# Pooling sums moved behind their matrix product, squares summed on the tensor engine, row roots on GpSimd, and eight FFN weight units kept for both token halves

## The reference, cut to what matters

```python
gate = sigmoid(rms_norm(h, g_ple) @ w_ple_gate + b_ple_gate)     # 512 tokens, 1024x1024
h = h + gate * (p @ w_ple_proj)                                  # 256x1024
hs = concat(meta_tokens, h)                                      # 16 + 512 = 528 tokens
h = rms_norm_2(hs, norm_mix_pre[0])
# pool_mixer: 4 channel groups of 256, windows W = 2, 4, 8, 16
cs = cumsum(h);  p_g = (cs - cs shifted by W) / count - h        # over the tokens
mix = concat(p_g @ w_groups[g]) * scale                          # 4 products 256x256
hs = hs + rms_norm_2(mix, norm_mix_post[0])
h = rms_norm_2(hs, norm_ffn_pre[0])
hs = hs + rms_norm_2((silu(h @ w_gate) * (h @ w_up)) @ w_down, norm_ffn_post[0])   # 1024 -> 2816 -> 1024
```

## Time and profile before

| | |
|---|---|
| median of 3 runs | 2180.49 us (2180.46 to 2183.39) |
| the profiled execution | 2178.2 us, its span 2176.1 us |
| PE busy | 1931.7 us, 89% of the span |
| DVE / ACT / POOL busy | 1001.9 / 659.5 / 205.9 us |
| granted TensorE clock, mean | 0.942 of full speed |

### The profile page before, as it was taken

One profiled execution on the slowest core, in us unless ns is written; L12 is line 12 of the kernel. 1 busy time (PEld: TensorE's weight loads), 2 busy tenths in 40 slices (PEclk: granted clock), 3 DMA queues, 4 the chain that ended last, 5 costly groups with the idle time before them and its releaser, 6 DMA issues.

```text
span 2176.1 us, 32437 instructions
## 1 busy us (share of the span) xinstructions
PE 1931.7 (89%) x13854; PEld 1649.0 (76%) x13854; DVE 1001.9 (46%) x1798; ACT 659.5 (30%) x1215; POOL 205.9 (9%) x205
## 2 busy tenths in 40 slices
PE   5987999949999989988569999997988969999997
PEld 4754788836665656668569999997856759999996
DVE  5744334342333322347884422447655485322456
ACT  5333323211100010034443222234454543222232
POOL 0021000000000000001230000003122240000012
PEclk9998999959999999998779999998989979999998
DMA  4211243539999999941114232233301224232242
GB/s 151 87 40 56 82 142 139 207 151 406 426 425 425 426 425 426 425 196 59 31 57 146 88 102 84 88 117 108 106 30 59 78 83 141 98 107 84 92 140 84
DMA packets 59236, 359.92 MB, mean 165 GB/s; under 512 B 6432, under 2 KB 9120, under 8 KB 46800
## 3 DMA queue, kind: packets, MB, share of 16 engines
q1 hardware_dynamic: 55120, 344.22, 41.6%
q0 software_dynamic: 3504, 12.73, 1.6%
q10 hardware_dynamic: 464, 0.85, 0.1%
HBM read 353.58 MB, written 4.19 MB: 164 GB/s over the span
## 4 chain that ended last, share of the span: by engine, by line
PE 68%; DVE 12%; DMA 10%; ACT 5%; POOL 2%; issue 2%; SPq 0%; POOLq 0%; DVEq 0%; ACTq 0%
PE bank L402 49%; DMA e<-in_we 9%; PE bank L587 7%; PE bank L609 4%; ACT SS L2184 1%; POOL zacc L2292 1%; PE bank L448 1%; PE bank L620 1%; DVE ztmp L1494 1%; DVE wlo L988 1%; PE bank L621 1%; DVE scr L1151 1%; DMA B<-in_rel 1%; DVE SS L1631 1%; DVE sm L1638 1%
## 5 line engine op out<-in xcount | busy, mean ns | idle before, releaser
L402 PE MATMUL bank<-nhi,whi 128*128 128x256 f32 (+2 forms) x1568 | 457.4, 292 | 21.9 <-DVE nlo L1504 7.7
L402 PE MATMUL bank<-nlo,whi 128*128 128x256 f32 (+2 forms) x1568 | 451.8, 288 | 0.0
L402 PE MATMUL bank<-nhi,wlo 128*128 128x256 f32 (+2 forms) x1568 | 451.6, 288 | 0.0
L988 DVE TENSOR_TENSOR wlo<-raw,whi 128x1024 fp32r<-128x1024 f32 x259 | 323.6, 1255 | 138.8 <-ACT whi L1745 135.0
L402 PEld LDWEIGHTS bank<-nhi,whi 128*128 128x128 f32 x1568 | 302.2, 193 | 28.0 <-issue 13.6
L1745 ACT CAST whi<-raw 128x1024 fp32r<-128x1024 f32 x259 | 269.4, 1042 | 121.7 <-PE bank L402 101.4
L402 PEld LDWEIGHTS bank<-nhi,wlo 128*128 128x128 f32 x1568 | 301.6, 192 | 1.6
L402 PEld LDWEIGHTS bank<-nlo,whi 128*128 128x128 f32 x1568 | 301.9, 193 | 1.0
L587 PE MATMUL bank<-e,xT 128*64 128x256 f32 x2048 | 237.1, 385 | 1.0 <-DVE xT L1280 1.0
L587 PEld LDWEIGHTS bank<-e,xT 128*64 128x64 f32 x2048 | 143.1, 138 | 83.0 <-issue 12.8
L402 PE MATMUL bank<-ghi,whi 128*128 128x256 f32 (+1 forms) x704 | 201.1, 286 | 0.0
(11 more groups left out here) (281 smaller groups left out, 2837.0 us busy)
## 6 DMA issues: line engine op xcount, KB each, us to landing
e<-in_we SPq DMA_DIRECT2D x96, 2048.0 KB, 36.6
raw<-in_w_down SPq DMA_DIRECT2D x64, 512.0 KB, 3.4
raw<-in_w_gate SPq DMA_DIRECT2D x52, 512.0 KB, 3.4
raw<-in_w_up SPq DMA_DIRECT2D x52, 512.0 KB, 3.5
raw<-in_w_q SPq DMA_DIRECT2D x12, 512.0 KB, 4.5
B<-in_rel POOLq DMA_DIRECT2D x8, 512.0 KB, 4.2
raw<-in_w_gc SPq DMA_DIRECT2D x8, 512.0 KB, 4.0
raw<-in_w_ga SPq DMA_DIRECT2D x8, 512.0 KB, 4.3
```

The source lines that it names most:

```text
L402: i = e.matmul(o, a, x[:, k0 + k, c0:c1], start=(k == 0 and n == 0), stop=(k == j.K - 1 and n == 2))
L988: e.tensor_tensor(wlo[wslot(u)][:], raw[u % NRAW][:], whi[wslot(u)][:].bitcast(F32), ALU.subtract).then_inc(*hit("dve_low", ("lo", u)))
```

## The change

It does these things:
- **Windows behind the product.** `pw` now multiplies the split of `hT` times the gain, without the factor; DVE applies the factor to the product on its way out of PSUM (`scaled_products`), and makes the window sums of the product into `yT` (`windows`). The window sums are linear, so the result is the same; `pool_scale` goes into the gain of the following norm (`gp`).
- **An explicit order** of 16 gate tiles j on all engines, without a break between the halves, with the pooling products of half 0 after tiles 12 to 15 (PSUM banks 4, 5, 6 in turn; bank 7 takes column sums).
- **Squares on TensorE** for `ple` 0, `pre0` 1, `mp0` and `fp0` (`SUMMED`): `square_sum` multiplies each block's squares by ones, one matmul per block and chunk, in place of the additions on POOL and the closing `columns`. POOL still adds for `ple` 1 and `pre0` 0.
- **Root on POOL** for all eight norms here (`root_of`), with the mean made by ACT (`mean`).
- **Weights kept**: the 8 units of the first FFN tiles are loaded and split once and used by both halves (`SLOT`, twelve slots); half 1's `fg`, `fu` are the same jobs as half 0's.
- **Post of `mp0`** in both halves is a block of its own (`mixed_post`) with all adds on DVE; `pe_open` writes out the order of the first FFN tiles. Two table loads of ACT are placed ahead of their use (`warm`). The spread of the last expert pair comes after `pp` tile 1, not 3.

```diff
-                if m == 3:
-                    pe_spread(NP - 1, range(8), w, pool=SIDE)
-            side.add(pe_norm("ple", 0, 4, 6))
-            side.add(nothing(8))
-            side.add(pe_norm("ple", 1, 4, 6))
...
+                if m == 1:
+                    pe_spread(NP - 1, range(8), w, pool=(4, 5, 2, 3, 6, 7))
+                if m > 4:
+                    for k in (2 * m - 10, 2 * m - 9):
+                        square_sum("ple", 0, k)
+            side.add(sums("ple", 0, (6, 7)))
+            for j in range(16):
+                r, m = j // 8, j % 8
+                tile(J["pg"], m, ("pg", m, r), phi[r], plo[r], [(0, (0, 256))], lambda k: [("pn", k, r)], keep=(r == 0))
+                if j == 0:
+                    side.drain()
+                if j == 1:
+                    spread("ple", 0)
+                if j == 5:
+                    columns("ple", 1)
+                if j == 7:
+                    side.add(spread_in(3, "ple", 1))
+                if j == 8:
+                    side.drain()
+                if j == 10:
+                    columns("pre0", 0)
+                if j > 10:
+                    square_sum("pre0", 1, j - 11)
+                if j == 11:
+                    side.add(spread_in(3, "pre0", 0))
+                if j == 12:
+                    side.drain()
+                if j >= 12:
+                    pool_products(0, (2 * j - 24, 2 * j - 23), REST)
...
         def pe_pool():
-            columns("pre0", 1)
...
+            for k in range(5, 8):
+                square_sum("pre0", 1, k)
+            pool_products(1, range(4), DENSE)
+            pool_products(1, (4, 5), REST)
+            spread("pre0", 1)
+            for k in range(8):
+                square_sum("mp0", 0, k)
+            pool_products(1, (6, 7), DENSE)
+            spread("mp0", 0)
+
+        def pe_open():
...
             for r in range(2):
+                side.add(sums("fp0", r, range(4 * r, 8)))
+                for i in range(FIRST):
+                    tile(J["fg", 0, i, r], 0, ("fg", 0, i, r), nhi, nlo, [(r, RG[r])], lambda k: [("n", "fp0", r, k)],
+                         keep=(r == 0))
+                    side.drain()
+                    tile(J["fu", 0, i, r], 0, ("fu", 0, i, r), nhi, nlo, [(r, RG[r])], lambda k: [], keep=(r == 0))
+                    if i == 0:
+                        spread("fp0", r)
+                    if r == 0 and i == 1:
+                        for k in range(8):
+                            square_sum("mp0", 1, k)
+                    if r == 0 and i == 2:
+                        spread("mp0", 1)
+                    if r == 0 and i == 3:
+                        for k in range(4):
+                            square_sum("fp0", 1, k)
+
+        def square_sum(nm, r, k):
...
+            for x, c in chunks:
+                n = MT if x == 0 and k else 128
+                p = e.matmul(b[0:n, x:x + 1], sq[:, c - c0:c - c0 + n], ones[:, 0:1], start=(k == 0 and x == chunks[0][0]),
+                             stop=(k == 7 and x == chunks[-1][0]))
...
+            for m in (2 * g, 2 * g + 1):
...
+                e.tensor_tensor(zn[:, m, MT:MT + n], bk("pw", m, r, 0, n=n), rb[:, c0:c1], ALU.mult).then_inc(
+                    *hit("dve_win", ("free", "pw", m, r, 0)))
...
+        def dve_pool():
             for g in range(4):
+                scaled_products(1, g)
+            windows(1, 0)
+            windows(1, 1)
+            mixed_post(0)
+            windows(1, 2)
+            windows(1, 3)
+            feed(U_FFN + 4)
...
         def act_pool():
+            mean("pre0", 1)
+            feed(U_FFN + 2)
+            pooled_squares(0, range(4))
             rb_copy("pre0", 1)
+            pooled_squares(0, range(4, 8))
+            mean("mp0", 0)
+            feed(U_FFN + 4)
+            mixed_post(0)
+            mean("fp0", 0)
+            pooled_squares(1, range(4))
+            rb_copy("fp0", 0)
...
+        def root_of(nm, r):
...
+            e.tensor_scalar(y.bitcast(I32), xm.bitcast(I32), -0.5, 1597463007.0, ALU.mult, ALU.add).then_inc(*hit("pool_root"))
+            for n in range(3):
+                w.wait_ge(*last("pool_root"))
+                e.tensor_tensor(u, y, y, ALU.mult).then_inc(*hit("pool_root"))
+                w.wait_ge(*last("pool_root"))
+                e.tensor_tensor(u, u, xm, ALU.mult).then_inc(*hit("pool_root"))
+                w.wait_ge(*last("pool_root"))
+                e.tensor_scalar(u, u, -0.5, 1.5, ALU.mult, ALU.add).then_inc(*hit("pool_root"))
+                w.wait_ge(*last("pool_root"))
+                e.tensor_tensor(y, y, u, ALU.mult).then_inc(*hit("pool_root"))
...
+            for i in range(m0, n1):
+                e.tensor_scalar(dg[:, i - 1, :], ident, rcol[:, 0, i:i + 1], None, ALU.mult).then_inc(
+                    *hit("pool_root", *([("diag", nm, r)] if i == n1 - 1 else [])))
...
+        for nm, r in (("ple", 0), ("ple", 1), ("pre0", 0), ("pre0", 1), ("mp0", 0), ("fp0", 0), ("mp0", 1), ("fp0", 1)):
+            if (nm, r) not in SUMMED:
+                for k in range(1, 7):
+                    accumulate(nm, r, k)
+            root_of(nm, r)
```

More of the change, by code:

```diff
@@ L687, in nothing, with spread_in @@
                 yield
-        def pe_pool():
-            columns("pre0", 1)
-            for r in range(2):
-                for m in range(8):
-                    tile(J["pw"], m, ("pw", m, r), nhi, nlo, [(0, RG[r])], lambda k: [("win", k, r)],
-                         k0=2 * (m // 2), keep=(r == 0))
-                    if r == 0 and m == 3:
-                        spread("pre0", 1)
-                if r == 0:
-                    side.add(pe_post("mp0", 0))
-            side.drain()
+        def spread_in(n, nm, r):
+            yield from nothing(n)
+            spread(nm, r)
+            yield
@@ L701, in columns, with sums @@
+        def sums(nm, r, ks):
+            for k in ks:
+                square_sum(nm, r, k)
+                yield
         def columns(nm, r):
             c0 = RNG[nm][r][0]
-            b = take(("col", nm, r), SIDE)
+            b = take(("col", nm, r), (7,) if nm in ("ple", "pre0") else SIDE)
             w.wait_ge(*at("acc", nm, r, 6))
             w.wait_ge(*at("sq", nm, r, 7))
-            sq = zlast[marks.noted("last", nm, r)]
+            sq = zq[marks.noted("sq", nm, r, 7)]
             for x, c in CH[r].items():
@@ L716, in spread @@
             m0 = max(n0, 1)
-            b = take(("rb", nm, r), SIDE)
+            b = take(("rb", nm, r), REST if nm in ("ple", "pre0", "mp0", "fp0") else SIDE)
             o = MT if n0 == 0 else 0
@@ L742, in pe_ffn @@
             rdy = [lambda k, r=r: [("n", nev, r, k)] for r in range(2)]
-            for r in range(2):
+            if l == 0:
+                pe_open()
+            for r in range(2) if l else ():
                 for i in range(FIRST):
@@ L910, in tensor @@
         pe_pool()
-        side.add(pe_norm("fp0", 0, 2, 4))
-        side.add(pe_post("mp0", 1))
-        side.add(pe_norm("fp0", 1, 2, 6))
         pe_ffn(0, RG, 0, "fp0", pe_after0)
@@ L922, in _program, with span @@
     WAIT = 10
+    SUMMED = [("ple", 0), ("pre0", 1)] + [(n, r) for n in ("mp0", "fp0") for r in range(2)]
+    def span(r):
+        return RG[r]
     LAG = (4, 6)
@@ L1446, in win_low @@
[L1446 to L1468 removed]
+            n = c1 - c0
@@ L1735, in scalar @@
         fed, nsq = [0], [0]
[L1736 removed]
+        sq_user = {}
         def feed(top):
@@ new lines, in act_ple, with act_gate_step @@
+            for i in (15, 16):
+                act_gate_step(i)
+            e.activation(warm[:], epst[:], ACT.Silu).then_inc(*hit("act_route"))
+        def act_gate_step(i):
+            if i < 16:
+                sigmoid(i % 8, i // 8)
+            if 0 <= i - 1 < 16:
+                k, r = (i - 1) % 8, (i - 1) // 8
+                c0, c1 = span(r)
+                w.wait_ge(*at("h ple", k, r))
+                e.activation(nhi[:, k, c0:c1], hT[:, k, c0:c1], ACT.Copy, scale=v1("mix_pre", k)).then_inc(
+                    *hit("act_norm", ("win hi", k, r)))
+                square("pre0", r, k, hT)
@@ L2030, in act_pool, with pooled_squares, mixed_post @@
+        def pooled_squares(r, ks):
+            for k in ks:
+                w.wait_ge(*at("pooled", k // 2, r))
+                square("mp0", r, k, yT, v1("pool_scale", k))
+        def mixed_post(r):
+            rb_copy("mp0", r)
+            for _ in post_steps("mp0", r, "fp0", ("ffn_pre", 0), 0):
+                pass
         def act_pool():
+            mean("pre0", 1)
+            feed(U_FFN + 2)
+            pooled_squares(0, range(4))
             rb_copy("pre0", 1)
-            side.add(nothing(8))
@@ L2033, in act_pool @@
-            for m in range(8):
-                tile(J["pw"], m, cap=J["pw"].u0 + 1)
-                c0, c1 = RG[0]
-                w.wait_ge(*at("out", "pw", m, 0))
```

(16 more changed lines are left out.)

461 lines of the change are left out of this document (231 added, 230 removed), and 4 rows, old and new, of the table k.

## The result

The changed kernel takes 2165.98 us (median of 4 runs, 2163.63 to 2166.57), the kernel before 2180.47 us (4 runs, 2178.53 to 2183.39) beside it. The ratio is 0.993, with a 95% interval from 0.9913 to 0.9948. It is faster, by 14.5 us; the forecast was 43 us, and its range ended at 2163. One execution of the kernel before (4774.87 us, beside experiments 1 to 4) and one of experiment 3 (3981.70 us) fell in another, much slower state of the chip and are in no figure here.

The account below looks back on a forecast made before the run. TensorE's stream bounds the kernel outside a hole of idle time and half clock. Milestones won 51.5 us at full clock, less 8 clock loss: 43.5 off 2178.2 is 2134.7, written as a 2138 us median; range 2120 to 2163.

Parts of the forecast that it names:

- the forecast's milestones: PE's predicted times: `pg` 974.1, end of `pw` half 0 1033, first FFN tile 1055.5, first tiles done 1121 at full clock.
- its clock loss of 8: Half clock in parts from 1033 to 1066 costs 3 to 14 us, taken as 8.
- the 8 where I had the cover end: `ple` 1 and `mp0` 1 have three tiles of cover, gone from about 8 us a root on.
- The forecast's waits of PE for diagonals: PE's waits for roots up to the first 528-token tile: 1, 1.7, 3.2, 2 and 1 us.
- the price of the root: A root on POOL: small instructions at 0.25 us each, 4 us in all, between bounds of 3.2 and 9.7.
- its count of six places: Six roots stand in PE's way: `ple` 0, `pre0` 0 and 1, `mp0` 0, `fp0` 0 and 1.
- it keeps the clock up: The added square matmuls, 18.5 us at full clock, land much in idle time of PE and keep its clock up.
- the upper bound: POOL's root at large-addition pace: 13 instructions at 0.61 us and 3 diagonals at 0.6, 9.7 us.
- the forecast's own rule: Each us more in a root on POOL costs 6 us, for six roots in PE's way.
- The rival on the slow POOL: Small POOL instructions cost like large ones, 0.61 us, root 9.7 us: 2180 us, no gain; chance 0.09.
- the post of `mp0` paces `fg` 0: In the first FFN tile, DVE's three instructions a block set the pace: 1.17 us a block, 9.4 in all.
- Worth nothing themselves: The eight weight units less save no time themselves, since PE never idles after 1136.9 us.

Follow-up runs that it names:

- experiments 1 to 4: Changed kernel with, in turn: one Newton step, 2148.15 us; roots back on DVE, 2161.96; squares of `mp0`, `fp0` added on POOL, 2168.87; column sums left out, 2154.56.
- experiment 3: Changed kernel with the squares of `mp0` and `fp0` added on POOL again, roots left there: 2168.87 us.
- after: The changed kernel itself, as timed beside the kernel before: 2165.98 us, ratio 0.993.
- experiment 1: Changed kernel with one Newton step instead of three in POOL's eight roots: 2148.15 us.
- experiment 4: Changed kernel without the column matmuls of blocks 1 to 6 in `mp0` and `fp0`: 2154.56 us.
- Number 7: Changed kernel with one Newton step in POOL's roots and the column sums of blocks 1 to 6 in `mp0`, `fp0` left out: 2138.03 us.
- experiment 8: Changed kernel with ScalarE's reciprocal square root and diagonals in place of mean, root and diagonals on POOL: 2150.30 us.
- number 9: Changed kernel with roots on ScalarE, and six norms' sums made with ones standing still and squares moving: 2128.48 us.
- experiment 5: Changed kernel with 16 unused matmuls ahead of each of four PE waits for a diagonal: 2163.02 us.
- experiment 6: Changed kernel with the kept weights undone, 8 units loaded, subtracted and cast again for half 1: 2174.0 us.

## Why the prediction was right in kind and wrong in size

Here are the forecast's milestones and those of the traces (start of `pg`, last `pw` matmul of half 0, start of the first FFN tile, start of the first 528-token tile; us of the span; the forecast's last with its clock loss of 8), and the medians:

```
kernel                     pg      pw half 0   first FFN   528-token   median
forecast                   974.1   1033        1055.5      1129        2138
after                      976.5   1046.7      1081.5      1162.8      2165.98
1, one Newton step         975.3   1038.2      1064.6      1141.3      2148.15
4, sums left out           975.1   1045.3      1075.0      1150.0      2154.56
7, both                    975.2   1038.1      1061.0      1131.3      2138.03
8, root on ScalarE         976.4   1040.5      1064.6      1145.4      2150.30
9, wide sums too           974.9   1037.1      1057.9      1125.4      2128.48
```

**Right.** The waits for POOL's additions went, and with them the windows between `scaled` steps. DVE's steps are fast with POOL's additions away, as the forecast took from the earlier trace rows: a post's split of 128x272 takes 0.49 us in number 9. PE's two waits for DVE are as forecast: 3.8 us for the first post (4 with the copy) and 2.2 for a bank (2.3). `ple` 1 and `mp0` 1 were covered, though `mp0` 1's root took 7.6 us, near the 8 where I had the cover end.

**Where the stretch went.** From the start of `pg` to the first 528-token tile the forecast has 154.9 us and the trace 186.3, 31.4 more. The forecast's waits of PE for diagonals are 8.9 us (1, 1.7, 3.2, 2 and 1), the measured ones 17.9: 9.0 more. Its clock loss is 8 us, the measured one about 29 by the estimate below: 21 more. The other terms make 1 to 2 us. So two steps of the forecast failed, the price of the root with its count of six places, and "it keeps the clock up" with the 8 us of loss that stood on it; the clock is the larger one.

**Root on POOL: mis-sized.** The step read: "A few elements are nearer to the memset, so I take 0.25 each, 4 us." By itself a small step is 0.19 us with a pitch of 0.275, as taken; but a 128x128 diagonal is 0.6, as the upper bound had it, and beside DVE's two-input instructions a small step lasts until they end, 0.3 to 1.2 us. So the isolated root is 4.8 and the six are 6.6 in the mean. 2.6 us more at six places is 15.6 us by the forecast's own rule, and the rule has two places too many: at the first four the roots are 13.6 us longer than 16, and PE's waits 11.6 longer than the forecast's; at `fp0` 0 and 1 the `fu` 0 tile, slow at the low clock, hides the root, and the waits are 0.5 us where the forecast had 3. The rival on the slow POOL is this mechanism, halfway.

**Column sums in the post: the step that named the wrong pace.** The forecast said that "the post of `mp0` paces `fg` 0", 9.4 us in all, and priced column matmuls at 0.22 in it. At the low clock a block's weight matmuls take 0.96 us (1085.40 to 1086.36) and its three sums 1.01 (to 1087.37), and PE, at 1.97 us a block, is the pace and not DVE at 1.17: 6.4 us more over 8 blocks. By the forecast's prices at the full clock, the block would be 1.04 us and DVE the pace; it is the clock that turned this over. The 24 sums of `mp0` 0 took 8.84 us in place of 5.3, the 16 of `mp0` 1 4.9 in place of 3.5. These three make 11.3 us, and they are part of the clock's loss below, not beside it. That leaving 60 such matmuls out won 11.4 (experiment 4) is another quantity: it takes away most of the sums, and gives half of that back in waits.

**"It keeps the clock up": wrong.** This was said of the added squares. The granted clock fell to 0.53 under them. As an estimate, a busy us at a mean clock c lacks 1 - c of its work: from 976.5 to 1162.8 the rows above give 62.74 x 0.07, 20.41 x 0.30, 21.04 x 0.47, 28.21 x 0.13 and 29.29 x 0.16, together 29 us, where the forecast allowed 8. The two terms and the clock are not three separate losses: with the root on ScalarE and the sums wide, the like stretches of number 9, from 975 to 1140, give 63.06 x 0.02, 11.57 x 0.26, 16.25 x 0.17, 15.48 x 0.09 and nothing from 1105 on, together 8.4 us, and so about the forecast's 8. Part of it is measured without that estimate: with the roots shorter the same matmuls took 8.2 us less of busy time (experiment 1), with the roots on ScalarE 4.9 less (experiment 8). How much the clock alone would give back isn't settled: filling four gaps gave 3 us, which can't be told from zero (experiment 5), and no run here held the clock up with all else the same.

**"Worth nothing themselves": wrong.** That is what the forecast said of the eight units less, since PE never idled after 1136.9. This is true of the order of before; in the new one, without the kept weights, the first tiles of half 1 come when their weights aren't cast and split, and they are worth 8.0 us (experiment 6), at least with the casts in the written order that was tried. It didn't move the forecast's sum, in which no weight was late.

**Number 7 lands on the forecast, but does less than it.** Root and sums shortened together win as much as was missed, 27.9 us. That doesn't share out the miss: it leaves 60 matmuls out that the forecast had priced at 13 us, and so other terms were short by about as much: `pw` of half 0 still ends 5 us later than forecast, of which 1.1 us are the later start, 1.3 are waits for the two roots in it beyond the 1 us counted (2.0 and 0.3), and 1.5 the low clock of its first 15 us (PE busy 12.79 us at 0.88). That the number is met so closely is in part luck; that the two terms add isn't.

## What to carry to other kernels

When a small serial step moves to another engine, price it beside what its neighbours will do at that moment, and give the instructions at its end (here the diagonals) their own price by their size; then add it up over the places where somebody waits for it, and look in the trace which these are: of the six here PE waited at four. Matmuls of one moving column are dear on TensorE, and the granted clock stayed low under them here; where a broadcast of the sum is wanted in the end, let the ones stand still and the squares move, and the sum, its mean, its diagonal and its spread become one matmul a block and one activation. A unit that is "never waited for" is so in the old order only: ask again in the new one.

## What the runs showed of the hardware

- POOL on 128x2 or 128x3 elements: 0.19 to 0.20 us, 0.275 apart. If a DVE instruction with two SBUF inputs runs beside it, the step ends 0.04 to 0.06 us behind that instruction: up to 0.49 us beside 128x256, 0.58 to 0.71 beside 128x512 to 128x572, 1.04 to 1.18 beside 128x1024. Beside DVE's instructions with an input in PSUM it keeps its 0.19 to 0.20. The effect goes both ways: DVE's split of 128x272 took 0.99 us beside POOL's additions. POOL's 128x128 scaling takes 0.59 us, and up to 1.07 beside DVE; ScalarE's takes 0.39.
- ScalarE's reciprocal square root of 128x272 from a bank takes 0.49 us, and its table load 1.28 us, mostly hidden by a one-column activation ahead of the wait (1.35 us of PE's wait at one place in number 8).
- TensorE busy throughout at the lower clock: 14.7 us without a gap in after, with three matmuls of 272 columns and three of one column in turn. With one matmul of 272 columns in place of the last three the clock rose within the same tile (number 9, at 1063.8).
